# A retention and expert-retrieval step on one core: the first two tiles crosswise behind 44 constant matmuls, and a first sum of squares on GpSimd

## What is computed

```python
def rmsnorm(x, g):
    return x * rsqrt(mean(x * x, axis=-1) + EPS) * g

h    = rmsnorm(x, norm_mix_g)              # x: 264 tokens of 2048
proj = h @ w_in                            # 2048 x 7168, cut into conv and retention parts
q, k = rotary(q), rotary(k)                # 8 heads of 128
o, s = retention(q, k, v, s0)              # chunks of 128, states written out
x    = x + concat(y_conv, y_ret) @ w_out
x    = x + peer(rmsnorm(x, norm_ffn_g))    # product keys, top 16, 16384 experts
y    = rmsnorm(x, norm_final_g)
```

## Time and profile before

| | us |
|---|---|
| median of 3 runs | 2108.09 |
| lowest and highest | 2107.91, 2108.57 |
| the profiled execution | 2108.31 |
| its span, first to last instruction | 2106.5 |

### The profile page before, as it was taken

The page is one execution under the profiler, slowest core; times in us unless marked ns, Lnnn a source line. Parts: engine busy times, 40 slices in busy tenths (PEclk is TensorE's granted clock), DMA queues, the critical chain, the costliest instruction groups (busy, mean ns, idle before and its releaser), DMA issues.

```text
span 2106.5 us, 46484 instructions
## 1 busy us (share of the span) xinstructions
PE 2085.1 (99%) x18585; PEld 2079.0 (99%) x18585; DVE 1440.8 (68%) x2701; ACT 961.2 (46%) x1343; POOL 68.6 (3%) x94
## 2 busy tenths in 40 slices
PE   8999999999999999999999999999999999999997
PEld 8999999999999999999999999999999999999997
DVE  8788876569988577754666666665645556666665
ACT  6666533445534344443434344444434344444444
POOL 1111000000000000000000000000000000000000
PEclk9999999999999999999999999999999999999999
DMA  8666555654455556675656565555655565655553
GB/s 297 222 217 217 194 180 182 201 180 156 166 190 180 180 187 215 214 243 182 201 192 216 194 207 199 201 205 195 207 196 200 180 213 207 213 202 205 206 178 125
DMA packets 115175, 418.39 MB, mean 199 GB/s; under 512 B 13600, under 2 KB 14112, under 8 KB 114752
## 3 DMA queue, kind: packets, MB, share of 16 engines
q1 hardware_dynamic: 100800, 365.29, 51.2%
q0 software_dynamic: 9888, 34.47, 5.0%
q10 hardware_dynamic: 4320, 16.22, 2.0%
HBM read 391.55 MB, written 24.29 MB: 197 GB/s over the span
## 4 chain that ended last, share of the span: by engine, by line
PE 97%; DVE 1%; DMA 0%; ACT 0%; issue 0%; DVEq 0%; SPq 0%; ACTq 0%
PE bank L940 31%; PE bank L942 31%; PE bank L941 31%; PE bank L1113 2%; DVE wlo L1192 1%; PE bank L1068 1%; DMA acc<-xT 0%; PE bank L1013 0%; ACT whi L640 0%; DMA raw<-halves 0%; DVE acc L1883 0%; PE bank L1024 0%; PE bank L1020 0%; ACT xghi L690 0%; PE bank L988 0%
## 5 line engine op out<-in xcount | busy, mean ns | idle before, releaser
L1192 DVE TENSOR_TENSOR wlo<-raw,whi 128x1024 fp32r<-128x1024 f32 x688 | 830.5, 1223 | 494.0 <-ACT whi L640 490.3
L640 ACT CAST whi<-raw 128x1024 fp32r<-128x1024 f32 x688 | 708.2, 1045 | 624.5 <-PE bank L942 619.1
L940 PE MATMUL bank<-xhi,whi 128*128 128x264 f32 x3200 | 912.4, 285 | 0.0
L942 PE MATMUL bank<-xlo,whi 128*128 128x264 f32 x3200 | 905.6, 283 | 0.0
L941 PE MATMUL bank<-xhi,wlo 128*128 128x264 f32 x3200 | 905.6, 283 | 0.0
L940 PEld LDWEIGHTS bank<-xhi,whi 128*128 128x128 f32 x3200 | 601.7, 188 | 0.0
L942 PEld LDWEIGHTS bank<-xlo,whi 128*128 128x128 f32 x3200 | 601.6, 188 | 0.0
L941 PEld LDWEIGHTS bank<-xhi,wlo 128*128 128x128 f32 x3200 | 600.8, 188 | 0.0
L940 PE MATMUL bank<-xghi,whi 128*128 128x264 f32 x1152 | 334.3, 290 | 9.1 <-DVE wlo L1192 9.1
L940 PE MATMUL bank<-wexp_hi,whi 128*128 128x264 f32 x1152 | 328.4, 285 | 0.0
L942 PE MATMUL bank<-xglo,whi 128*128 128x264 f32 x1152 | 327.3, 284 | 0.0
(11 more groups left out here) (217 smaller groups left out, 1124.9 us busy)
## 6 DMA issues: line engine op xcount, KB each, us to landing
raw<-halves SPq DMA_DIRECT2D x688, 512.0 KB, 3.6
hid<-gates ACTq DMA_DIRECT2D x30, 528.0 KB, 4.7
gates<-stage POOLq DMA_DIRECT2D x17, 768.0 KB, 7.3
s_old<-ret_state POOLq DMA_DIRECT2D x8, 512.0 KB, 7.1
vs_all<-values POOLq DMA_DIRECT2D x8, 512.0 KB, 5.6
ret_sample<-s_new POOLq DMA_DIRECT2D x8, 512.0 KB, 4.2
gates<-route_mem POOLq DMA_DIRECT2D x5, 768.0 KB, 7.4
acc<-xT SPq DMA_DIRECT2D x4, 528.0 KB, 6.8
```

Of the source, the lines that this page charges most:

```text
L640: nc.scalar.copy(whi[:, s], raw[:, s]).then_inc(hi_done, 1)
L940: nc.tensor.matmul(back, whi[:, s, c], high, start=start and c == 0, stop=False)
L942: mm = nc.tensor.matmul(back, whi[:, s, c], low, start=False, stop=stop and c == HALF - 1)
L1192: v.tensor_tensor(wlo[:, s], raw[:, s], whi[:, s].bitcast(F32), ALU.subtract).then_inc(lo_done, 1)
```

## The change

Seven things change, all at the start of the program.

1. TensorE first runs 44 matmuls of 264 columns on a bf16 tile of ones (`filler`, the memory of `i1T`), into bank 7, which is not read. They wait only for a memset of that tile on VectorE.
2. Tiles 0 and 1 run crosswise (`first_tiles`): first halves of both (chunks 0 to 7 of x) into banks 0 and 1, then second halves of both (chunks 8 to 15). The four halves are loaded in the order 0, 2, 1, 3.
3. SyncE's order is x0, half, x1, half, x2, half, x3, half, `keep`.
4. ScalarE and VectorE split a half behind each block of four chunks of x.
5. GpSimd squares chunks 0 to 7, two at a time, and sums them: four multiplications and three additions of 528 columns, each behind a semaphore of the one before. They stand ahead of the tables' loads. The sum is in `early`, in memory of `outer` and `s_rest`.
6. ScalarE squares only chunks 8 to 15. VectorE sums those with three instructions of 528 columns (there were seven for all 16 chunks) and adds `early` with a fourth, behind semaphore `early_ready`.
7. Since tile 0 now ends with the third half, `values_out` of head 0 waits for that.

```diff
@@ SyncE
             def first_half(s):
-                sp.dma_start(raw[:, s], halves[s]).then_inc(raw_full[s], 16)
+                sp.dma_start(raw[:, s], halves[FIRST_HALVES[s]]).then_inc(raw_full[s], 16)
             x_block(1)
+            first_half(1)
             x_block(2)
-            first_half(1)
+            first_half(2)
             x_block(3)
-            first_half(2)
+            first_half(3)
             sp.dma_start(keep[:], consts[:, 0:KEEP]).then_inc(keep_in, 16)
-            first_half(3)
@@ GpSimd
+            step = Chain(pool, early_step)
+            for c in range(0, HALF, 2):
+                if c % 4 == 0:
+                    pool.wait_ge(x_in[c // 4], 16)
+                two = acc[:, c:c + 2, :]
+                step.did(nc.gpsimd.tensor_tensor(early_two if c else early, two, two, ALU.mult))
+                step.wait()
+                if c:
+                    last = nc.gpsimd.tensor_tensor(early, early, early_two, ALU.add)
+                    if c < HALF - 2:
+                        step.did(last)
+                        step.wait()
+                    else:
+                        last.then_inc(early_ready, 1)
             pool.wait_ge(x_in[3], 16)
             pool.dma_start(tables[:], consts[:, KEEP:NCONST]).then_inc(consts_in, 16)
@@ ScalarE
                 if c == 3:
                     hi_half(0, 0)
+                if c == 7:
+                    hi_half(0, 1)
                 if c == 11:
-                    hi_half(0, 1)
+                    hi_half(0, 2)
@@ TensorE
+            def first_tiles():
+                waits = norm_waits(0)
+                for s in range(2):
+                    some = slice(s * HALF, (s + 1) * HALF)
+                    for k in range(2):
+                        half(0, 2 * s + k, bank[k][:, 0:T], [xghi[:, c, :] for c in range(CH)[some]],
+                             [xglo[:, c, :] for c in range(CH)[some]], s == 0, s == 1, waits[s] if k == 0 else ())
...
+            pe.wait_ge(filler_set, 1)
+            for _ in range(WARM_UP):
+                nc.tensor.matmul(bank[7][:, 0:T], filler[:, 0:P], filler[:, T:2 * T], start=True, stop=True)
@@ VectorE
             v.memset(warm[:, 0:1], 1.0).then_inc(warm_set, 1)
+            v.memset(filler, 1.0).then_inc(filler_set, 1)
@@ VectorE, first_norm
+                dve.wait_ge(early_ready, 1)
+                dve.wait_ge(sq_used, CH - 1)
+                v.tensor_tensor(pair[:], pair[:], early, ALU.add).then_inc(sq_used, 1)
                 lo_half(0, 5)
```

More of the change, by code:

```diff
@@ L44 @@
 RING = 4
+FIRST_HALVES = (0, 2, 1, 3)
+WARM_UP = 44
 BANKS = 4
@@ L703, in _ @@
                     hi_half(0, 0)
+                if c == 7:
+                    hi_half(0, 1)
                 if c == 11:
[L705 removed]
+                    hi_half(0, 2)
             def first_squares():
[L708 removed]
                 hi_half(0, 3)
[L710 to L716 removed]
+                for c in range(HALF, CH):
+                    if c >= HALF + SQ_RING + 2:
+                        act.wait_ge(sq_used, c // 2 * 2 - 2)
+                    place = squares[:, c % SQ_RING] if c > HALF + 1 else pair[:, c - HALF]
+                    nc.scalar.activation(place, acc[:, c, :], ACT.Square).then_inc(sq_ready, HALF + 1 if c == HALF else 1)
+                    if c == HALF + 3:
                         hi_half(0, 4)
@@ L1031, in head @@
                         part(h - 1)
-                    if tiles:
-                        tile(r, k, h, k, xghi, xglo, norm_waits(0) if first and k == 0 else ({}, {}),
+                    if first and k < 2:
+                        if k == 0:
+                            first_tiles()
+                    elif tiles:
+                        tile(r, k, h, k, xghi, xglo, ({}, {}),
                              (lambda: sum_over_partitions(1)) if first and k == 2 else None)
@@ L1240, in first_norm @@
             def first_norm():
-                for c in range(2, CH, 2):
+                for c in range(HALF + 2, CH, 2):
                     dve.wait_ge(sq_ready, c + 2)
-                    if c > 2:
+                    if c > HALF + 2:
                         dve.wait_ge(sq_used, c)
                     two = squares[:, c % SQ_RING:c % SQ_RING + 2]
-                    if c == 2:
+                    if c == HALF + 2:
                         v.scalar_tensor_tensor(out=pair[:], in0=pair[:], scalar=EPS * D / P / 2, in1=two,
-                                               op0=ALU.add, op1=ALU.add).then_inc(sq_used, 4)
-                    else:
-                        v.tensor_tensor(pair[:], pair[:], two, ALU.add).then_inc(sq_used, 2)
-                    if c == HALF - 2:
-                        lo_half(0, 4)
+                                               op0=ALU.add, op1=ALU.add).then_inc(sq_used, HALF + 4)
+                        lo_half(0, 4)
+                    else:
+                        v.tensor_tensor(pair[:], pair[:], two, ALU.add).then_inc(sq_used, 2 if c < CH - 2 else 1)
+                dve.wait_ge(early_ready, 1)
+                dve.wait_ge(sq_used, CH - 1)
+                v.tensor_tensor(pair[:], pair[:], early, ALU.add).then_inc(sq_used, 1)
                 lo_half(0, 5)
@@ L1361, in values_out @@
             def values_out(h):
-                tile_done(h * 2, 0)
-                if not (isinstance(h, int) and h == 0):
+                if isinstance(h, int) and h == 0:
+                    dve.wait_ge(half_used, 3)
+                else:
+                    tile_done(h * 2, 0)
                     dve.wait_ge(values_saved, h * 16)
@@ L1373, in head @@
                 tiles, att, norm = steps_of(h)
-                if loads_tiles(h):
+                if first:
+                    lo_half(0, 3)
+                elif loads_tiles(h):
                     ahead(r, 0)
```

17 lines of the change are left out of this document (9 added, 8 removed).

## The result

| | before | after |
|---|---|---|
| median, us | 2108.24 (17 executions) | 2112.26 (17) |
| lowest and highest | 2107.71, 2108.94 | 2111.22, 2117.73 |
| the profiled execution, its span | 2108.31, 2106.5 | 2112.99, 2111.2 |

The ratio is 1.0021, with a 95% interval of 1.0015 to 1.0028. The forecast was 2106.6; the kernel got 4 us slower instead of 1.7 us faster. That is less than the 0.2% that the prediction calls clear of noise, but the interval excludes 1. The profiled execution lies 0.7 us above its median, so its trace shows a little more loss than the median has.

What follows compares the result with a forecast made beforehand. TensorE, busy 99% of the span, was taken as the bound; a faster half 0 and crosswise halves start half 4 at 21.2 instead of 22.92, so -1.7 us on 2108.31 gives 2106.6; range 2105.8 to 2113.6.

Steps and rivals of the forecast that it cites:

- rival 1: GpSimd and VectorE take turns at the start, delaying the first four halves; 2110 to 2115 us, chance 0.32.
- Its price of 1.07 us: Time for each of GpSimd's seven 528-column instructions, taken by the column from VectorE's slowest two-input row; range 0.71 to 2.08.
- Its path: With strict turns all seven GpSimd instructions precede the fourth half's low part, at 24.6; half 4 starts 4.6 us later.
- The clock within rival 1: If TensorE's clock falls while it idles among the first halves, 20 matmuls at 0.218 add up to 2 us.
- the end of the constants: Constant matmuls start at about 1.3 and end at 8.6, before half 0 starts at 9.05, hidden in an existing wait.
- Everything else is ready: Behind the first halves, VectorE's sums and low parts come before TensorE asks; half 9's load is 1.7 to 2.3 us earlier.
- The crosswise order: In the first halves: at full speed half 0 ends at 12.0; the old order would wait 2.1 us for half 1.
- The raised clock: Half 0's first 20 matmuls run at 0.121 instead of 0.218 us each, costing 1.9 us less.
- The arrivals of x: Loads at the start, 1.38 us for each large transfer: x1 at 8.54, x2 at 11.3, x3 at 14.1.
- GpSimd's sum: GpSimd's seven instructions take 8.2 us from x0 at 5.12 to 13.3; VectorE wants their sum at 21.7.
- Rival 3: GpSimd's code reload lasts past 13.5, making `early` late; a reload to 18 gives about +3, 2111; chance 0.06.
- Rival 4: Constant matmuls don't raise the clock or run past 9.05; half 0 ends near 14; 2108 to 2110, chance 0.04.

Runs made afterwards that it cites:

- the squares left out: Changed kernel without GpSimd's seven instructions, chunks 0 to 7 missing from the norm, 9 further constant matmuls behind half 0's cast; 2108.56 us, ratio 1.0002.
- gated constants: Changed kernel without GpSimd's squares (ScalarE and VectorE do all 16 chunks), 9 further constant matmuls waiting for half 0's cast; 2108.02 us, ratio 0.9999.

## Why the prediction was wrong, step by step

**The step that failed** is the choice between the forecast and rival 1. The forecast let GpSimd's seven instructions run beside VectorE's at no cost, on the ground that no row showed otherwise. No row of before had both engines computing, so the trace was silent, and silence was read as "they don't disturb each other". What the runs showed in its place: they take turns, instruction by instruction, and that adds 5.9 us to VectorE's rows. The low part of the second half, forecast for 12.5, was done at 17.17. The page of the Trainium skill named above, SBUF — State Buffer, section "SBUF: two separate sides", spoke against it. Rival 1 was given 0.32 where it should have been the likeliest. The time of 2112.26 lies in the stated range only because rival 1 was given room in it.

**How far rival 1's working held.** Its mechanism did, and its range of 2110 to 2115. Its price of 1.07 us was 1.06 to 1.14 for a multiplication and 1.38 for an addition of two tiles. Its path did not: it had TensorE wait for the low part of the fourth half until 24.6, while that was done at 22.68 (21.46 + 1.22) and nobody waited for it. TensorE waited before half 0 and in the middle of it, until 15.29, and from there its own 0.22 us a matmul set the pace until 20.5. With 72 constants the clock stays up, and half 4 is 3.4 us late and not 4.9. So 4.6 (worked out without the clock) beside 4.94 (measured with it) is in part luck.

**The clock within rival 1** held as well, "up to 2": it is about 1.6 by the traces of the run with 72 constants, about 1 by the medians. The prediction tied the end of the constants (8.6, measured 9.24; they started at 1.52 and not 1.3, since the memset took 0.50, and 9.24 is past 9.05, which cost nothing only because that low part was late) to a low part at 9.05. They bridge nothing when that low part is late. Nor is their end fixed: the same 44 ended between 7.94 and 9.24 in the traces, as their matmuls came to 0.12 apart after 12 to 25 of them.

**"Everything else is ready"** failed too, unseen behind the first error. Without contention, and with half 4 at 21.18, k moved 0.1 us. The prediction let the load of half 9 land as much earlier as it was issued. With the squares left out it was issued 3.24 us earlier (22.94) and took 7.00 us for 3.89; half 8's cast starts at 28.70 and half 9's at 29.96, against 28.67 and 30.09 before. The cause fits the DMA engines, which have nothing free (the earlier trace rows has them at 1.02 until 25.80, the row above at 1.02 until 28). A chain of waits shows the order of things, not how far each can move.

**What held.** The crosswise order was needed for the constants to be worth anything: without it half 1 still started at 14.20. The raised clock is worth what was forecast: with gated constants the sum over the partitions started 1.4 us earlier, with the squares left out 1.7. The arrivals of x didn't hold anything up; x1 was there by 7.67 and not 8.54, which the forecast had not reckoned with. GpSimd's sum was in time and the tables' load went out at 14.88 (14.1 forecast). Rival 3 did not happen: GpSimd started at 5.08 with x0, with no delay for its code. The Trainium skill, GPSIMD Engine Reference, section 2.1, gives about 6 us for a first call; no row here shows one. GpSimd waited 4.6 us for x0, so a reload of up to that length could have hidden there; by the page's figure, as an estimate, one that begins with that wait at 0.46 would have ended near 6.5, later than the first multiplication started. Rival 4 did not happen as told: the clock rose, and 44 constants in 7.72 us are near the 7.3 us that the prediction gives them (20 at 0.218 and 24 at 0.121).

**What stays open.** Why head 0's first `s_new` starts 0.5 us later than `outer` allows in three kernels (the first that leaves squares out, the one with the state load on SyncE's queue besides, and the one with GpSimd's squares alone), and not in the others; and why four of eleven executions with the state load on SyncE's queue are 2 to 6 us longer. For the two longest of these (2114.42 and 2114.02) the mean granted clock is 0.996 where the others have 0.998, so TensorE's clock has a part in them; no trace shows which wait came before that.

## What to carry to other kernels

When work is moved to an idle engine, ask what it shares with the engine it is meant to relieve. Arithmetic and copies on GpSimd kept VectorE's two-input arithmetic out until they ended here, so they must stand where VectorE waits, or not be there; a trace in which both never compute together is no evidence for either. A gain near a program's start must then be followed through the next loads: where the DMA engines were full, a load asked for 3.24 us earlier landed 0.13 us earlier, and a large load that was held back held up what stood behind it. And each wait of TensorE that a change leaves open can cost its clock besides its own length.

## What the runs showed of the hardware

- Of GpSimd's instructions on 128x528, multiplications (1.06 to 1.14 us) and additions (1.38) stretched VectorE's low parts from 0.49 to as much as 1.54 us, and a half's from 1.23 to 2.32. Copies (0.71) stretched them to 0.85 and 1.64. In all three a low part ended 0.28 to 0.29 us behind the end of GpSimd's instruction. Memsets (0.54) did nothing, and ScalarE beside them was never slowed (1.73 for four). GpSimd itself was held up too: 1.93 for a multiplication that takes 1.14.
- Constant bf16 matmuls raise TensorE's clock, from 0.22 to 0.12 us a matmul, but it fell again behind 1.83 and 3.37 us of idle time, and not behind 0.67, 0.97 or 1.10, nor behind the 1.34 us in front of half 0 in the kernel with memsets.
- A transfer of 4 KB issued right behind one of 512 KB in GpSimd's queue released its successor 5.0 to 7.3 us after its issue (four traces), against 2.1 to 4.0 in the sixteen others.
- Where the DMA engines had no time free, a 512 KB load issued at 22.94 took 7.00 us; the same load issued at 26.18 in the kernel before took 3.89.
